# A mixture-of-experts trunk: who waits for a block's scatter, and what the router reads for the last token tile

## The reference, cut to what matters

```python
for l in range(DEPTH):                      # 2 layers, 1024 tokens, D = 1024
    h = rms_norm(x, norm1_gain[l]); z = h @ w_in[l]
    ...                                     # dilated attention on q, k, v; pooling on u
    x = x + concat([att, pool]) @ w_out[l]
    x = x + hier_moe(rms_norm(x, norm2_gain[l]), ...)

def hier_moe(h, ...):                       # router: h @ w_group + b_group, h @ w_router + b_router
    ...                                     # best group of 4, best 2 experts of 4 inside it
    a = silu(h @ w_gate[e]) * (h @ w_up[e]) * gate
    y = a @ w_down[e]                       # each token: sum over its 2 experts
```

## Time and profile before

| | |
|---|---|
| median of 3 runs (lowest, highest) | 1689.78 us (1686.36, 1689.96) |
| the profiled execution, its own time | 1689.52 us |
| its span in the trace | 1687.7 us |
| busy: PE, DVE, ACT, POOL | 84%, 59%, 40%, 20% |
| scatters `out_x<-x_res,arena` (line 686), issue | 62, mean 1806 ns |
| gathers `x_res<-token_rows` (line 672), issue | 62, mean 1241 ns |
| expert loop, layer 0 and layer 1 | from 557 to 794 us and from 1373 to 1619 us |

### The profile page before, as it was taken

One profiled execution on the slowest core, in us unless ns is written; L12 is line 12 of the kernel. 1 busy time (PEld: TensorE's weight loads), 2 busy tenths in 40 slices (PEclk: granted clock), 3 DMA queues, 4 the chain that ended last, 5 costly groups with the idle time before them and its releaser, 6 DMA issues.

```text
span 1687.7 us, 24335 instructions
## 1 busy us (share of the span) xinstructions
PE 1425.3 (84%) x7323; PEld 1147.1 (68%) x7324; DVE 1000.1 (59%) x1917; ACT 670.1 (40%) x1028; POOL 342.4 (20%) x204
## 2 busy tenths in 40 slices
PE   5999978998993799997599998899899749999930
PEld 4887867887883566774478786788778636776610
DVE  6777666663445666665566866666534476666620
ACT  4232145663211465664422224557412125655510
POOL 1000059002000122333310003910200012222331
PEclk9999989999996799998799999989999859999975
DMA  8000020000138599974652002000012936999644
GB/s 317 22 1 0 0 101 1 2 1 13 74 138 285 168 315 331 336 208 62 165 100 106 0 0 100 1 1 1 13 42 83 332 108 157 333 286 338 164 65 73
DMA packets 115873, 204.46 MB, mean 121 GB/s; under 512 B 9816, under 2 KB 76576, under 8 KB 115776
## 3 DMA queue, kind: packets, MB, share of 16 engines
q1 hardware_dynamic: 90976, 130.77, 22.5%
q0 software_dynamic: 19136, 53.67, 14.7%
q10 hardware_dynamic: 5664, 18.88, 2.8%
HBM read 169.72 MB, written 49.28 MB: 130 GB/s over the span
## 4 chain that ended last, share of the span: by engine, by line
PE 72%; DMA 9%; DVE 8%; issue 7%; ACT 3%; ACTq 1%; DVEq 0%; POOLq 0%; POOL 0%; PEld 0%; SPq 0%; PEldq 0%
PE ps L1496 16%; PE ps L1707 15%; PE ps L1476 10%; PE ps L1629 9%; PE ps L1722 9%; DMA out_x<-x_res,arena 7%; PE ps L1582 7%; PE ps L1556 2%; PE ps L1558 2%; PE ps L1643 2%; DVE arena L1257 1%; PE ps L1616 1%; DVE w_in_lo L1050 1%; DMA big<-in_w_in 1%; DVE k_high L1137 1%
## 5 line engine op out<-in xcount | busy, mean ns | idle before, releaser
L1362 DVE TENSOR_TENSOR gu_lo<-big,gu_hi 128x2048 fp32r<-128x2048 f32 x96 | 219.3, 2293 | 116.9 <-ACT gu_hi L896 106.2
L1476 PE MATMUL ps<-cst,arena 128*128 128x128 f32 x1242 | 188.4, 286 | 84.4 <-DVE arena L1021 35.9
L1476 PEld LDWEIGHTS ps<-cst,arena 128*128 128x128 f32 x1242 | 153.7, 147 | 131.4 <-DVE arena L1021 37.8
L1496 PE MATMUL ps<-w_in_hi,hT_hi 128*128 128x512 f32 x512 | 205.6, 402 | 13.3 <-DVE hT_lo L1039 10.5
L1496 PE MATMUL ps<-w_in_hi,hT_lo 128*128 128x512 f32 x512 | 201.8, 394 | 0.0
L1496 PE MATMUL ps<-w_in_lo,hT_hi 128*128 128x512 f32 x512 | 201.5, 394 | 0.0
L896 ACT ACTIVATE gu_hi<-big 128x2048 fp32r (+1 forms) x96 | 183.9, 1918 | 35.8 <-PE ps L1707 35.8
L686 POOL DMA_INDIRECT out_x<-x_res,arena x62 | 112.0, 1806 | 317.9 <-issue 249.7
L1722 PE MATMUL ps<-big,arena 128*128 x360 | 163.8, 598 | 4.4 <-issue 4.4
L672 POOL DMA_INDIRECT x_res<-token_rows,row_tok x62 | 76.9, 1241 | 443.7 <-issue 332.2
L1158 DVE CUSTOM_DVE_ANT_0 arena<-ps,cst 128x128 f32<-128x128 f32 (+7 forms) x128 | 96.8, 756 | 102.6 <-PE ps L1558 102.1
(11 more groups left out here) (180 smaller groups left out, 2308.0 us busy)
## 6 DMA issues: line engine op xcount, KB each, us to landing
big<-in_w_gate SPq DMA_DIRECT2D x32, 1024.0 KB
big<-in_w_up SPq DMA_DIRECT2D x32, 1024.0 KB
big<-in_w_down SPq DMA_DIRECT2D x32, 1024.0 KB, 14.4
big<-in_w_in SPq DMA_DIRECT2D x14, 1024.0 KB, 9.9
big<-in_w_out SPq DMA_DIRECT2D x4, 2048.0 KB, 10.1
token_rows<-arena ACTq DMA_DIRECT2D x16, 512.0 KB, 3.3
out_x<-x_res ACTq DMA_DIRECT2D x16, 512.0 KB, 4.0
x_res<-out_x SPq DMA_DIRECT2D x8, 512.0 KB, 4.4
```

The source lines that it names most:

```text
L1362: ve.tensor_tensor(out=gu_lo[i], in0=raw, in1=gu_hi[i].bitcast(f32), op=ALU.subtract)\
L1476: ins = te.transpose(ps[:, bank + i // 4, (i % 4) * P:(i % 4 + 1) * P], src, ident)
L1496: ins = te.matmul(ps[:, 2 + 2 * par_ + i, :], a[par_][:, k, :], b[:, k, :], start=k == 0 and n == 0, stop=k == K - 1 and n == 2)
```

## The change

Two things are changed. First, the wait for landed scatters moves. Before, GpSimd waited in `add_rows(j)` until scatters 0 to j-1 had landed, then counted `y_free`, which let ScalarE and VectorE write `y` of block j+1. Now `y_free` is gone; ScalarE itself waits in `moe_down(t)` for scatters 0 to t-1, VectorE's `y_evac(t)` waits for ScalarE's copy of block t-2, and GpSimd waits only for the two copies. For blocks that are not used nobody waits for `s_add`. ScalarE's copy `aT(t)` also moves ahead of `moe_down(t-1)`.

Second, for tile 7 of the out projection TensorE transposes `xr` itself as soon as `x_upd` is counted; VectorE applies the gain when it copies the result out of PSUM (two instructions with the gain broadcast) and the token's factor in `add_bias`. `add_bias` becomes a SCALAR_TENSOR_TENSOR for every tile.

```diff
                 def add_rows(j):
-                    if j:
-                        pool.wait_ge(s_add, upto_added(l, j))
-                    pool.sem_inc(y_free, 1)
                     pool.wait_ge(y0_ready, upto(l, BLOCKS, j + 1))
...
                 def moe_down(t, slot, m):
                     a_.wait_ge(dn_done, upto(l, BLOCKS, t + 1))
-                    a_.wait_ge(y_free, upto(l, BLOCKS, t + 2 - RING))
+                    if not first(t):
+                        a_.wait_ge(s_add, upto_added(l, t))
+                        a_.sem_inc(s_passed, 1)
                     sc.activation(y[slot][:, 512:1024], ps[:, 5, :], ACT.Copy).then_inc(y1_ready, 1)
...
+                    a_.wait_ge(a_t_done, upto(l, BLOCKS, t + 1))
+                    sc.activation(aT, ps[:, 3, 0:FE].rearrange("p (k c) -> p k c", c=P), ACT.Copy).then_inc(aT_ready, 1)
                     if not first(t):
                         moe_down(t - 1, *before(slot, m))
-                    a_.wait_ge(a_t_done, upto(l, BLOCKS, t + 1))
-                    sc.activation(aT, ps[:, 3, 0:FE].rearrange("p (k c) -> p k c", c=P), ACT.Copy).then_inc(aT_ready, 1)
...
                 def y_evac(t, slot, m):
                     dve.wait_ge(dn_done, upto(l, BLOCKS, t + 1))
-                    dve.wait_ge(y_free, upto(l, BLOCKS, t + 2 - RING))
+                    dve.wait_ge(y1_ready, upto(l, BLOCKS, t + 2 - RING))
...
                 def add_bias(t, par_):
-                    ve.tensor_tensor(out=R("lg", NR)[:, ds(t, 1), :],
-                                         in0=ps[:, 6 + par_, 0:NR].unsqueeze(1),
-                                         in1=par[:, BIAS_R:BIAS_R + NR].unsqueeze(1), op=ALU.add).then_inc(logits, 1)
+                    ve.scalar_tensor_tensor(out=R("lg", NR)[:, ds(t, 1), :],
+                                            in0=ps[:, 6 + par_, 0:NR].unsqueeze(1),
+                                            scalar=st[:, 8 + par_:9 + par_] if last(t, T) else 1.0,
...
                 def gain2(t, par_):
+                    if last(t, T):
+                        times_gain(h2T[par_], par[:, G2:G2 + K], 4, h2T_ready)
+                    else:
...
                 def xt2(t, par_):
-                    pe.wait_ge(xs2_ready, upto(l, T, t + 1))
+                    if last(t, T):
+                        pe.wait_ge(x_upd, upto(l, T, T))
+                    else:
+                        pe.wait_ge(xs2_ready, upto(l, T, t + 1))
...
-                    transposes(4, cols(xs2[par_], K)).then_inc(xt2_done, 1)
+                    transposes(4, cols(xr[:, T - 1, :] if last(t, T) else xs2[par_], K)).then_inc(xt2_done, 1)
```

More of the change, by code:

```diff
@@ L309, in trunk @@
         gates_listed = sem("gates_listed")
-        y_free = sem("y_free")
         spare_may = sem("spare_may")
@@ L585, in _ @@
             pool.wait_ge(s_ms, 2)
-            for s in (x_ready, pooled, wo_split, y_free):
+            for s in (x_ready, pooled, wo_split):
                 pool.sem_inc(s, BIAS)
@@ L1209, in add_bias @@
                     dve.wait_ge(rt_done, upto(l, T, t + 1))
-                    ve.tensor_tensor(out=R("lg", NR)[:, ds(t, 1), :],
-                                         in0=ps[:, 6 + par_, 0:NR].unsqueeze(1),
-                                         in1=par[:, BIAS_R:BIAS_R + NR].unsqueeze(1), op=ALU.add).then_inc(logits, 1)
+                    ve.scalar_tensor_tensor(out=R("lg", NR)[:, ds(t, 1), :],
+                                            in0=ps[:, 6 + par_, 0:NR].unsqueeze(1),
+                                            scalar=st[:, 8 + par_:9 + par_] if last(t, T) else 1.0,
+                                            in1=par[:, BIAS_R:BIAS_R + NR].unsqueeze(1), op0=ALU.mult,
+                                            op1=ALU.add).then_inc(logits, 1)
                 def gain2(t, par_):
                     dve.wait_ge(xt2_done, upto(l, T, t + 1))
-                    ve.tensor_copy(h2T[par_], ps[:, 4:6, :].rearrange("p a (k n) -> p (a k) n", n=P)).then_inc(h2T_ready, 1)
+                    if last(t, T):
+                        times_gain(h2T[par_], par[:, G2:G2 + K], 4, h2T_ready)
+                    else:
+                        ve.tensor_copy(h2T[par_], ps[:, 4:6, :].rearrange("p a (k n) -> p (a k) n", n=P)).then_inc(h2T_ready, 1)
                 def cat_low(t, par_):
@@ L1235, in out_dve @@
                                          in1=xr[:, t, :], op=ALU.add).then_inc(x_upd, 1)
+                    if last(t, T):
+                        add_bias(t - 1, 1 - par_)
+                        gain2(t, par_)
                     dve.wait_ge(sd2, upto(l, T, t + 1))
@@ L1242, in out_dve @@
                                             op0=ALU.mult, op1=ALU.mult).then_inc(xs2_ready, 1)
-                    if not first(t):
+                    if not (first(t) or last(t, T)):
                         add_bias(t - 1, 1 - par_)
                 steps(dve, T, out_dve, ch)
-                gain2(T - 1, (T - 1) % 2)
                 add_bias(T - 1, (T - 1) % 2)
```

## The result

| | before | changed kernel |
|---|---|---|
| median (lowest, highest) | 1688.37 us (1686.36, 1689.96), 4 runs | 1667.9 us (1659.16, 1669.5), 4 runs |
| ratio | | 0.9869, 95% interval 0.9831 to 0.9907 |
| profiled execution, its span | 1689.52, 1687.7 us | 1669.46, 1667.6 us |

The forecast was 1671.0 with a range of 1652 to 1693. The difference of the medians is 20.5 us (1.2%), that of the two spans 20.1; the forecast had 18.6. I read the profile after in the order of the prediction's terms.

A forecast was written before the change was run, and what follows sets the result against it. The prediction took TensorE to bound the expert loop, and scatters waited for one by one to bound the program's end and layer 0's end. 1689.5 - 29.6 - 4 - 13 + 28 = 1670.9, so 1671 us, range 1652 to 1693.

The forecast's parts named there:

- the tail: End of the program: unused blocks' scatters, no longer waited for one by one, overlap up to the DMA engines' limit; gain 29.6 us.
- start of layer 1: Tiles 5 to 7 no longer wait for layer 0's scatters, which are packed; gain 4 us, ends -2 and 10.
- router, both layers: Last router tile: earlier transposes and TensorE staying at its upper clock level; gain 6.5 us a layer, 13 in all.
- expert loop: ScalarE's copy waits for the previous scatter to land, slowing the loop while weights stream; cost 28 us, range 14 to 36.
- rival (c): End of the program: the scatters do not overlap and stay 6 us each; gain only 9 us, total 1692, chance 0.09.
- Rival (b): End of the program: GpSimd's issue, not the DMA, is the limit; gain 37 us, total 1663, chance 0.08.
- free limit: Expert loop, period 10.0 us: ScalarE's wait costs nothing while a scatter lands under 8.1 us after its issue.
- factor 10/12: Expert loop: saturated time is set by megabytes, so a period of 12 holds 10/12 as many blocks; 33.5 becomes 28 us.
- Rival (a): Expert loop: the wait is hidden, with landings under 8.1 us; total 1643, chance 0.10.
- rival (d): Expert loop: landings stay at their worst, 10.9 us, and the loop costs 65 us; total 1708, chance 0.12.
- `aT` first: Expert loop: copying `aT` ahead of the output copy is worth nothing, as it takes 0.38 us and is wanted 6 us later.

The follow-up runs named there:

- after_at_last: The changed kernel with ScalarE's copy `aT` put back behind the output copy; 1667.62 us, ratio 0.9889 to the kernel before.
- gpsimd_waits_too: The changed kernel with GpSimd's wait for landed scatters put back ahead of every scatter, unused blocks too; 1702.41 us, ratio 1.011 to the kernel before.
- router_only: The kernel before with only the router part of the change, scatter waits as before; 1677.17 us, ratio 0.9926.
- gu_first: The changed kernel with ScalarE's weight copy for block t+2 ahead of the output copy of block t-1; 1673.16 us, ratio 0.9926 to the kernel before.
- the light loads: The changed kernel and unused_free, each loading only 128 of 1024 gate and up rows for experts 4 to 15; layer 0 loops 215.9 and 212.2 us.
- after_bounded: The changed kernel with a bounds check on the scatter, so spare rows are not transferred; 1650.29 us, ratio 0.9786 to the kernel before.
- scatter_only: The kernel before with all edits of the change except the router part; 1680.86 us, ratio 0.9952.
- at_first: The kernel before with only ScalarE's copy `aT` moved ahead of the output copy; 1690.46 us, ratio 1.0026.
- unused_free: The kernel before with the router part, and GpSimd's wait skipped for unused blocks; 1640.76 us, ratio 0.9713.

## Why the prediction was right

The ledger, in microseconds of the profiled spans. "All else" is what is left of the sum, worked out before rounding.

| step of the prediction | forecast | measured |
|---|---|---|
| the tail | -29.6 (8 to 37) | -33.8 |
| start of layer 1 | -4 (-10 to 2) | -4.9 |
| router, both layers | -13 | -14.2 |
| expert loop | +28 (14 to 36) | +33.2 |
| all else | 0 | -0.5 |
| sum | -18.6 | -20.1 |

The terms and their signs were right. That the sum is off by only 1.5 us is in part luck: the tail gave 4.2 more than forecast, and the loop took 5.2 more. "All else" is a sum of the same kind: layer 0's first scatter comes 5.1 us sooner, 2.0 less than the router's gain there, and the stretch from the fixed point to layer 1's first scatter is 9.5 us shorter, 2.5 more than the router's gain. Neither is explained. (The forecast's own range is also added wrongly at its lower end: its terms give 1689.5 - 37 - 4 - 13 + 14 = 1649.5, not 1655. Nothing hangs on it.)

**The tail.** Right in kind: the scatters overlap, which refutes rival (c). The size was off by 4.2 us, and the term is the 3.4 us of all DMA engines for each scatter, taken from a window with one scatter in it. Packed, the share is 0.97 x 19 + 0.74 x 12 = 27.3 us for nine scatters and three gathers, so that a scatter has 3.0 at most; from the times, (1664.7 - 1635.44 - 6.2) / 8 = 2.9 (the 2.9 us behind the last landing kept). Rival (b) had GpSimd's issue as the limit, with 37, and the truth lies between. The trace of after_at_last tells each landing of the same tail. While gathers stand between the scatters, GpSimd's issue sets the pace: the scatters start 3.2 to 3.4 us apart and land 6.2 to 7.5 us behind their issue. The last six, issued 1.87 us apart, land 2.5 to 2.9 us apart (five distances, four of them 2.5), and the time from issue to landing grows from 6.8 to 10.2 us: there the DMA engines are the limit. So a scatter alone takes some 2.5 us of them, and 2.9 is the mean with gathers and starts between. The page that stood on the rival's side, the Trainium skill, DMA: Bandwidth & Descriptors, section on the anatomy of a SWDGE transfer, gives an estimate of 1.2 us of data for 512 KB. The trace disagrees: 2.5 us at least.

**The start of layer 1.** Forecast 4, measured 4.9. The other kernels bear out the size: with GpSimd alone waiting for every scatter the fixed point comes 134.1 to 136.9 us behind the last used scatter (three kernels, mean 135.7), without that wait 128.7 to 133.4 (eight, mean 130.5). Kernels of one kind lie up to 4.7 apart, as much as the gain, so that only the means speak for it. ScalarE's wait for tile 5 went from 3.32 us to nothing, as forecast; that gpsimd_waits_too has the gain as well shows that a smaller lead is enough.

**The router.** Right term by term: transposes at 1.04, not 1.98, router at 2.05, and TensorE stayed at the upper clock level, 2.4 GHz (granted clock 1.00 from 519.9 to 522.9 us; before it was 0.50 from 523.1 to 526.8, behind a stand of 4.4 us). In router_only the same transposes and products take 1.04 and 2.05 us.

**The expert loop.** The mechanism was right: landing under load bounds the copies at L + 1.7 (forecast L + 1.9). On the changed kernel's chain it is 8.6 to 11.1 us (once 7.35) where weights stream; the forecast's free limit was 8.1. Shown by gu_first and gpsimd_waits_too (where the price is), by the light loads (22.1 us become 3.7 in layer 0) and by after_bounded. The size, 33.2, was 5 us over the forecast in this execution. Over the five kernels with ScalarE's wait and unbounded scatters the sum is 453.8 to 461.5, over the six others 427.9 to 430.2: a price of 24 to 34, with means 457.4 and 429.2 a price of 28. In each layer the five have means of 225.2 and 232.2, and the six 209.1 and 220.1: 16 and 12 us. The forecast's parts are (20.5 - 1.1) x 10/12 = 16.2 and (15.2 - 1.1) x 10/12 = 11.8. So the term was sized rightly in the mean, and the profiled execution of the changed kernel is at its upper end. The factor 10/12 in it, that the saturated time is set by megabytes, no run tests by itself. Rival (a), the hidden wait, fell, and so did rival (d), whose 65 was twice what was paid.

The same page of the Trainium skill, DMA: Bandwidth & Descriptors, section on queues, rings and completion order, has each DMA engine take its queues in turn, packet by packet. From that the prediction had an estimate of 9.6 us for a scatter beside a load and a period of 11.5. The trace agrees in the size: 9.64, 9.68, 9.67 and 9.91 us in the rows above, out of a spread of 8.6 to 11.1 on the whole chain, and a distance of 11.2 to 11.6. The 3.4 us in that estimate have turned out as 2.5 to 3.0, which gives 8.7 to 9.2 in its place.

**A second price, not settled.** In the changed kernel the second low half of the weights starts late at the end of some loop bodies, and `gate_up` then starts 12.1 to 12.8 us behind the one before (12.1 behind these rows). VectorE's timeline:

```profile
737.99 2.29 DVE L1367 TENSOR_TENSOR gu_lo<-big,gu_hi 128x2048 fp32r<-128x2048 f32 x1 [3.52 <-ACT gu_hi L892]
741.55 2.29 DVE L1367 TENSOR_TENSOR gu_lo<-big,gu_hi 128x2048 fp32r<-128x2048 f32 x1 [1.27 <-issue]
```

Between the first and the last used scatter, gaps of 0.9 to 3 us ahead of this instruction that no other engine ended are 3 in the kernel before, 9 in the changed kernel, 8 in after_at_last and in gpsimd_waits_too, 6 in scatter_only and none in gu_first. The sums of the loops of the last five are 461.5, 457.7, 457.3, 453.8 and 457.0. The kernel gu_first pays its price without a single such gap, so that they are not needed for it; whether they make up part of the 8 us by which the five kernels differ is not shown. No run took the gaps away alone.

**`aT` first, "worth nothing".** Right within 0.3%: at_first is 0.26% slower, a cost of some 4 us where none was given, and after_at_last leaves room for the same. What in ScalarE's order costs it is not settled.

## What to carry to other kernels

A wait costs by what its engine may still do while it waits. On GpSimd, with a spare buffer between it and the copies, landings of up to 11.2 us (unused_free) were free; the same wait on the copy that feeds the next scatter makes a ring of landing, copy and issue, and costs whatever the ring is over the period. Before such a wait is moved, take the landing time from the stretch where the weights stream, not from an empty tail, and look whether only some cases need it: skipping the wait for unused blocks alone gave the whole gain of the tail and none of the price (0.9713 together with the router part, and 0.9669 with the spare rows not transferred).

## What the runs showed of the hardware

- An accumulating scatter of 512 KB lands 6.2 us after its issue alone, and 8.6 to 11.1 us (once 7.35) on the changed kernel's chain beside weight loads; the longest in a loop is 12.1 (router_only).
- Back to back, with no gather between, scatters land 2.5 us apart (after_at_last), where a lone one shows a share of 0.49 over 7 us, 3.4 us. The share of a lone transfer overstates its cost in a row.
- With every row out of bounds a scatter still takes its 1.56 us of issue, and hardly any DMA time (a share of 0.02 at the end of after_bounded): the span then ends 5.8 us behind the last issue.
- Loading 1.25 of 3 MB for experts 4 to 15 made layer 0's loop of the old scheme 2.9 us longer (209.3 to 212.2), in one run, though its scatters landed sooner. The cause is open.
